# A hybrid attention and linear-attention step on one core: output projection in 512-column chunks, token groups outermost, each product split into two 64-row halves

## The reference, cut to what matters

```
def merge(x, o_attn, ga, o_gla, gg, gla_norm_g, w_out):
    o_gla = rmsnorm(o_gla...)
    mix = jnp.concatenate([o_attn * jax.nn.silu(ga), o_gla * jax.nn.silu(gg)], axis=-1)
    return x + mix @ w_out
```

## Time and profile before

| what | value |
|---|---|
| time, median of 3 runs | 2030.36 us (2029.29 to 2030.73) |
| profiled execution: span from first to last instruction | 2029.8 us |
| mean granted TensorE clock | 0.987 of full speed |
| PE busy | 1937.9 us (95% of the span), 12160 products |
| DVE, ACT, POOL busy | 835.3, 447.5, 640.0 us |
| DMA | 184.43 MB, mean 91 GB/s |

### The profile page before, as it was taken

How to read it: one execution, slowest core, us unless ns; L and a number is a source line. 1 busy time by engine, 2 the same in 40 slices (tenths; PEclk the granted TensorE clock), 3 DMA queues, 4 the chain that set the end, 5 groups by cost and what they waited for, 6 DMA issues and landing times.

```text
span 2029.8 us, 33101 instructions
## 1 busy us (share of the span) xinstructions
PE 1937.9 (95%) x12160; PEld 1809.8 (89%) x12160; DVE 835.3 (41%) x1553; ACT 447.5 (22%) x1064; POOL 640.0 (32%) x509
## 2 busy tenths in 40 slices
PE   5999999989999999999999999999999899999999
PEld 4899999867777779999988888889999899999999
DVE  6454453134334331111277777875555640000000
ACT  6211111133333331000244344441001120000000
POOL 1433333111112222233334434332323333333331
PEclk8999999989999999999999999999999999999999
DMA  6322222222222322221322222333433472222221
GB/s 214 128 65 65 65 65 75 78 69 75 71 68 75 96 64 88 71 71 56 92 76 84 75 83 75 86 96 120 143 110 107 142 233 88 88 86 81 86 88 34
DMA packets 237665, 184.43 MB, mean 91 GB/s; under 512 B 15345, under 2 KB 236017, under 8 KB 236178
## 3 DMA queue, kind: packets, MB, share of 16 engines
q1 hardware_dynamic: 159618, 131.99, 21.3%
q10 hardware_dynamic: 78000, 51.81, 9.1%
HBM read 133.27 MB, written 52.31 MB: 91 GB/s over the span
## 4 chain that ended last, share of the span: by engine, by line
PE 77%; DVE 13%; issue 4%; ACT 3%; DMA 2%; ACTq 1%; DVEq 0%; POOL 0%; SPq 0%; POOLq 0%
PE p L1557 14%; PE p L1559 14%; PE p L1558 14%; PE p L1631 7%; PE p L1632 7%; PE p L1633 7%; DVE xn L1723 4%; PE p L504 2%; PE p L487 2%; ACT work L551 2%; PE p L713 2%; PE p L497 2%; DVE work L627 1%; DVE work L613 1%; PE p L724 1%
## 5 line engine op out<-in xcount | busy, mean ns | idle before, releaser
L1557 PE MATMUL p<-x_hi,w_lo 128*128 128x384 f32 x2112 | 730.9, 346 | 0.0
L1559 PE MATMUL p<-x_hi,w_hi 128*128 128x384 f32 x2112 | 708.5, 335 | 0.0
L1558 PE MATMUL p<-x_lo,w_hi 128*128 128x384 f32 x2112 | 708.2, 335 | 0.0
L450 POOL TENSOR_TENSOR w_hi<-raw,small 128x512 fp32r<-128x512 f32 x176 | 186.3, 1059 | 870.9 <-PE p L1559 859.6
L1557 PEld LDWEIGHTS p<-x_hi,w_lo 128*128 128x128 f32 x2112 | 398.2, 189 | 41.6 <-issue 39.2
L1558 PEld LDWEIGHTS p<-x_lo,w_hi 128*128 128x128 f32 x2112 | 398.4, 189 | 0.4
L1559 PEld LDWEIGHTS p<-x_hi,w_hi 128*128 128x128 f32 x2112 | 397.8, 188 | 0.0
L1631 PE MATMUL p<-w_hi,x_lo 128*128 128x256 f32 x1152 | 328.2, 285 | 5.7 <-DVE x_lo L1796 5.7
L1632 PE MATMUL p<-w_lo,x_hi 128*128 128x256 f32 x1152 | 327.9, 285 | 0.0
L1633 PE MATMUL p<-w_hi,x_hi 128*128 128x256 f32 x1152 | 327.7, 284 | 0.0
L455 POOL TENSOR_TENSOR w_lo<-raw,w_hi 128x512 fp32r<-128x512 f32 x176 | 228.6, 1299 | 13.8
(11 more groups left out here) (181 smaller groups left out, 1842.7 us busy)
## 6 DMA issues: line engine op xcount, KB each, us to landing
raw<-in_w_in SPq DMA_DIRECT2D x176, 256.0 KB, 3.7
h_t<-xn SPq DMA_DIRECT2D x132, 192.0 KB, 1.9
raw<-in_w_out SPq DMA_DIRECT2D x32, 512.0 KB, 3.6
work<-h_t ACTq DMA_DIRECT2D x42, 256.0 KB, 5.2
out<-work ACTq DMA_DIRECT2D x76, 128.0 KB, 2.9
work<-h_t SPq DMA_DIRECT2D x24, 384.0 KB, 4.1
work<-h_t ACTq DMA_DIRECT2D x17, 512.0 KB, 5.6
work<-in_x_prompt SPq DMA_DIRECT2D x64, 128.0 KB, 3.5
```

The lines of the kernel that those rows point to most:

```text
L450: pool.tensor_tensor(w_hi[:, k:k + 4, 0:n], w_raw(k, n), zeros[:, :].unsqueeze(1) .to_broadcast([P, 4, n]), ALU.add).then_inc(s_whi, 1)
L1557: pe.matmul(out, w_lo[:, k, :], x_hi[:, k, tok], start=(k == 0), stop=False)
L1558: pe.matmul(out, w_hi[:, k, :], x_lo[:, k, tok], start=False, stop=False)
L1559: mm = pe.matmul(out, w_hi[:, k, :], x_hi[:, k, tok], start=False, stop=(k == KT - 1))
```

## The change: what it does

The chunk is 512 columns wide, so there are 4 chunks. The token groups are outermost: for each group of 384 tokens (three tiles) all 4 chunks are run, 12 group-chunks g in all, and the weights are loaded and split three times. The loads are per contraction slice: 128 x 512, 256 KB, in four slots, 192 loads. ACT makes the high part and DVE the low part, POOL has no more work here. Each product of 128 rows is issued as two of 64 rows, the lower and the upper half of the partitions, each into a PSUM bank of its own; a tile takes two banks, a group-chunk six, and they rotate over all eight. DVE adds first the one bank and the residual, then the other bank. The stores go through SP's queue, between the loads. All engines' code of this part is written out, without loops. The pieces of the activations come in the order of the groups: eight for the first group at the start, eight each for the second and third during g = 1 and g = 5.

```
-WCH = 256
+WCH = 512
+NGRP = NG * NCH
...
-            return [(q, n, i) for q in range(4) for n in range(NG) for i in range(2)]
+            return [(q, n, i) for n in range(NG) for q in range(4) for i in range(2)]
...
+        HALVES = [slice(0, P // 2), slice(P // 2, P)]
+        def half_bank(g, t, half):
+            return banks[(3 + 2 * NG * g + 2 * t + half) % 8][:, 0:WCH]
+        def piece_after(g, k):
+            if g % NCH == 1 and g // NCH + 1 < NG and 4 <= k < 12:
+                return 8 * (g // NCH + 1) + k - 4
+            return None
...
+                for k in range(4):
+                    load_w_out(0, k)
+                for t in range(NG):
+                    load_x_res(0, t)
+                load_pieces(4, 7)
                 store_last(0)
                 store_last(1)
-                load_pieces(4, 6)
+                load_pieces(7, 8)
...
+                for g in range(NGRP):
+                    for k in range(4 if g == 0 else 0, KT):
+                        load_w_out(g, k)
+                        if g == 0 and k == 5:
+                            store_last(2)
+                        if g > 0 and k == 6:
+                            for t in range(NG):
+                                store_y(g - 1, t)
+                                load_x_res(g, t)
+                        if piece_after(g, k) is not None:
+                            load_pieces(piece_after(g, k), piece_after(g, k) + 1)
...
+            def high_w(g, k):
+                u = 16 * g + k
+                act.wait_ge(t_w[k % 4], 16 * (u // 4) + 16)
+                if u < 4:
+                    act.wait_ge(s_wfree, 4 * N_ITEMS + (k + 5))
+                else:
+                    act.wait_ge(t_wfree, 2 * u - 6)
+                act.activation(o_hi[k % 4], o_raw[k % 4], ACT.Copy).then_inc(t_whi, 1)
...
-            high(0, 6)
+            high(0, 7)
+            for k in range(4):
+                high_w(0, k)
+            high(7, 8)
             item_silu(N_ITEMS, 2)
...
+            def out_chunk(n, g):
+                for b in range(4):
+                    for t in range(NG):
+                        if b == 0:
+                            pe.wait_ge(t_y, NG * g + (t + NG))
...
+                        for i in range(4):
+                            k = 4 * b + i
+                            if t == 0:
+                                pe.wait_ge(t_wlo, 16 * g + (k + 1))
+                                if k % 2 == 0:
+                                    pe.wait_ge(t_mlo, SLOTS + 8 * n + k // 2 + 1)
+                            for half, rows in enumerate(HALVES):
+                                pe.matmul(out[half], x_lo[rows, k, tok], o_hi[i][rows], start=(k == 0), stop=False)
+                            for half, rows in enumerate(HALVES):
+                                pe.matmul(out[half], x_hi[rows, k, tok], o_lo[i][rows], start=False, stop=False)
+                            for half, rows in enumerate(HALVES):
+                                mm = pe.matmul(out[half], x_hi[rows, k, tok], o_hi[i][rows], start=False,
+                                               stop=(k == KT - 1))
+                                if t == NG - 1:
+                                    mm.then_inc(t_wfree, 1)
+                                elif k == KT - 1:
+                                    mm.then_inc(t_acc, 1)
...
+            for g in range(NGRP):
+                for k in range(4 if g == 0 else 0, KT):
+                    if g > 0 and k == 0:
+                        add(g - 1, 0)
+                        add(g - 1, 1)
+                    low_w(g, k)
+                    if g > 0 and k == 3:
+                        add(g - 1, 2)
+                    if piece_after(g, k) is not None:
+                        low(piece_after(g, k), piece_after(g, k) + 1)
```

More of the change, by code:

```diff
@@ L241, in project @@
         t_mlo = sem("t_mlo")
-        t_w = [sem(f"t_w{i}") for i in range(2)]
+        t_w = [sem(f"t_w{i}") for i in range(4)]
         t_whi = sem("t_whi")
-        t_wready = sem("t_wready")
+        t_wlo = sem("t_wlo")
         t_wfree = sem("t_wfree")
-        t_x = [sem(f"t_x{i}") for i in range(NT)]
+        t_x = [sem(f"t_x{i}") for i in range(NG)]
         t_acc = sem("t_acc")
         t_y = sem("t_y")
+        t_y0 = sem("t_y0")
         t_st = [sem(f"t_st{i}") for i in range(3)]
@@ L367, in out_loads @@
                 sp.wait_ge(s_wready, 4 * (N_ITEMS + 1))
[L368 to L369 removed]
+                for k in range(4):
[3 more added lines that the diff above has]
+                load_pieces(4, 7)
                 store_last(0)
                 store_last(1)
[L372 removed]
+                load_pieces(7, 8)
                 sp.dma_start(o_dec, o_t[D_MODEL // 2:D_MODEL, SEQ:TOK].rearrange("(k p) n -> p k n", p=P))\
                   .then_inc(t_dec, 16)
[L375 to L388, removed]
+                for g in range(NGRP):
[10 more added lines that the diff above has]
+                for t in range(NG):
+                    store_y(NGRP - 1, t)
+                for t in range(NG):
+                    sp.wait_ge(t_st[t], 16 * NGRP)
             def store_item(j, row, n_rows, gates=None):
@@ L1394, in _ @@
                 split(pool, j)
[L1396 to L1409, removed]
         @block.scalar
@@ L1614, in _ @@
             pe.wait_ge(sl_og, 4 * NT + 1)
[L1615 to L1624, removed]
-                        for i in range(4):
[L1626 to L1638, removed]
@@ new lines, in out_chunk @@
+            def out_chunk(n, g):
+                for b in range(4):
+                    for t in range(NG):
+                        if b == 0:
+                            pe.wait_ge(t_y, NG * g + (t + NG))
+                        out = [half_bank(g, t, half) for half in range(2)]
+                        tok = slice(n * TN + t * P, n * TN + t * P + P)
+                        for i in range(4):
+                            k = 4 * b + i
[14 more added lines that the diff above has]
+                                    mm.then_inc(t_acc, 1)
@@ L1640, in _ @@
+            for n in range(NG):
+                for c in range(NCH):
+                    out_chunk(n, NCH * n + c)
         @block.vector
@@ L1809, in _, with low_w @@
-            dve.sem_inc(t_y, NT)
-            low(0, 6)
-            silu_g(N_ITEMS, 2)
[L1812 to L1817, removed]
+            def low_w(g, k):
+                dve.wait_ge(t_whi, 16 * g + k + 1)
+                if g == 0 and k < 4:
+                    dve.wait_ge(s_wfree, 4 * N_ITEMS + (k + 5))
+                dve.tensor_tensor(o_lo[k % 4], o_raw[k % 4], o_hi[k % 4].bitcast(F32), ALU.subtract)\
+                   .then_inc(t_wlo, 1)
@@ new lines, in add @@
+            def add(g, t):
+                if t == NG - 1:
+                    dve.wait_ge(t_wfree, 2 * (16 * g + KT))
+                else:
+                    dve.wait_ge(t_acc, 2 * ((NG - 1) * g + (t + 1)))
+                dve.wait_ge(t_x[t], 16 * g + 16)
+                if g > 0:
+                    dve.wait_ge(t_st[t], 16 * g)
+                dve.tensor_tensor(y_sb[:, t, :], half_bank(g, t, 0), x_res[:, t, :], ALU.add).then_inc(t_y0, 1)
+                dve.wait_ge(t_y0, NG * g + t + 1)
+                dve.tensor_tensor(y_sb[:, t, :], half_bank(g, t, 1), y_sb[:, t, :], ALU.add).then_inc(t_y, 1)
@@ new lines, in _ @@
+            dve.sem_inc(t_y, 2 * NG)
+            low(0, 7)
+            for k in range(4):
+                low_w(0, k)
+            low(7, 8)
+            silu_g(N_ITEMS, 2)
+            for g in range(NGRP):
+                for k in range(4 if g == 0 else 0, KT):
+                    if g > 0 and k == 0:
[4 more added lines that the diff above has]
+                        add(g - 1, 2)
+                    if piece_after(g, k) is not None:
+                        low(piece_after(g, k), piece_after(g, k) + 1)
@@ L1820, in hybrid_step @@
+            for t in range(NG):
+                add(NGRP - 1, t)
 def hybrid_step(nc, x_p, x_s, cache_k, cache_v, state, norm_g, w_in, w_up, b_gate, qg, kg, sinks, gla_g, w_out,
```

53 lines of the change are left out of this document (21 added, 32 removed).

## The result

The changed kernel takes 2064.57 us (median of 4 runs, 2060.75 to 2068.36), the kernel before 2029.82 beside it; the ratio is 1.0173, 95% interval 1.0153 to 1.0192. I had forecast 2014 us and a range up to 2046. The forecast had the wrong sign. One of the 13 executions of the kernel before that were taken beside three of the later runs took 3133.99 us at a mean granted clock of 0.556, and is left out of the ratios.

The account below looks back on a forecast made before the run. PE's product pace was taken to bound the kernel. Pace -41.5, start -1.8, pieces +16.3, clock +4.5, eighth slice +4.5 and end +1.3 sum to -16.7 from 2029.8: 2014 us forecast, range 1998 to 2046.

Parts of the forecast that it names:

- The pace: Output projection products: halves run side by side, 1728 pairs at 0.216 us take 373.2 us, 41.5 us less.
- my first rival: Output projection products: the fixed 0.0133 us stays on a pair, pace only 23.0 less, 2026 us; chance 0.25.
- The eighth slice: Chunk changes: its late load costs 0.5 us at nine changes, 4.5 us, plus 1.7 us twice in chunks with pieces.
- The clock: Blocks with pieces: three gaps over 2 us are each followed by low clock costing 1.5 us, 4.5 us together.
- The blocks with pieces: g = 1 and g = 5: pieces on DVE delay weight slots; 16.3 us, including 1.7 twice at the eighth slice.
- the gated block: Fourth block with pieces, which DVE multiplies, ACT casts and DVE subtracts: 2.85 us a slot, 6.3 us of waits.
- The end: After the last product: two adds instead of one and a store of twice the size, 1.3 us more.
- The start: Start of the output projection: PE starts 5.4 us after it was free, plus 3 us low clock; 1.8 us less.
- Late refills at every block: Start of each of 48 blocks: slot refill chain exceeds 0.28 us slack; at 0.7 us a block 2047 us; chance 0.18.
- no overlap: Output projection: halves of an fp32r product do not overlap, 3456 x 0.216 = 746 us, about 2350 us; chance 0.03.

Follow-up runs that it names:

- stores later: Changed kernel with three stores and three residual loads issued behind the eighth weight slice's load instead of ahead of it: 2024.58 us, ratio 0.998 to the kernel before.
- half of the queue: Changed kernel with only the three residual loads ahead of the eighth weight slice's load, the three stores behind it: 2032.22 us, ratio 1.0017 to the kernel before.
- one half alone: The kernel with stores later, pieces spread, with products of the lower half alone, contraction rows 64 to 127 left out: 2349.14 us in one execution.
- stores later, pieces spread: Stores later, plus 16 pieces of the second and third token group behind every fourth weight slice in two group-chunks each: 2005.97 us, ratio 0.9895.

## Why the prediction was wrong, step by step

**The pace** was the first wrong step. I took 0.216 us for a pair, "the nearest row in form", and it is 0.2267. The products of the earlier trace rows were like the new ones in their halves, those of the earlier trace rows in their type. In all rows here the fixed part goes with the type: fp32r pays 0.0133 at 256, 384 and 512 columns, at 128 rows and at 64. Why it does is open. The step was off by 18.5 us; this was my first rival, and with it alone I had 2026. The Trainium skill's formula ("TensorE: Matmul & The Clock Gate", section "Back-to-back issue gap") would give 0.2158 here; the trace does not agree. My own working with the two weight loads of a pair one after the other does not show either: they lie within 0.19 us (timeline).

```profile
1870.17 0.19 PEld L1655 LDWEIGHTS p<-w_hi,x_hi 64*128 64x128 f32 x2
```

**The eighth slice** was the larger one, and the one that turned the sign. The mechanism was named: its load stands behind the last add, three stores and three loads on SP. Its size was not: 7.9 us forecast, 30.2 measured. I issued it at 11.7 us after the start of the last block and landed it 2.9 to 3.7 us later; the eleven were issued at 12.6 to 14.5 and landed 5.4 to 9.4 later. In the gap whose chain is shown, the block began some 18.4 us ahead of 1889.0, when the eighth slice was due (two blocks and three slices at 0.2267), at 1870.6: the load is issued 12.8 us after it, and takes 5.92. The issue is late by another way than mine. I had SP wait for the last of the three adds and then issue two transfers. The last add ends at 11.1, before its store's turn at 11.5: what takes the time is the six transfers one after another behind slice 6, 3.3 us from 9.5 on. Each microsecond beyond the slack is paid eleven times. I had written "more if the 1.5 MB ahead of it are not through", took 0.5 us for nine changes, and gave the range only 1.5 us; it is 1.5 to 3.1 there, and 5.0 and 4.1 in the two chunks with pieces. The runs with the stores later and with half of the queue show this cause: issued at 9.85 us, the slice came in time, although it still took 5.1 us to land.

**The clock** was the same mechanism again: eleven gaps instead of three could drop it. It did so behind five of the eleven and at the gated pieces, for 15.1 us instead of 4.5. With the gaps at the eighth slice gone, 4.8 are left.

**The blocks with pieces** were about right: 10.0 us against 12.9 (11.35 with their share at the eighth slice), the gated block 5.6 against 6.3, and they went when the pieces were moved behind the fourth slice. **The end** was right. **The start**: the first gap was 6.7 us against 5.4, counted as in the prediction from the end of the input projection. Nearly all of the difference is the load of the seventh piece (number 6), which landed 4.7 us after its issue where I had taken 3.5. (The links that I listed behind it add up to 0.6 less than the time that I gave; DVE takes the low part of that piece first, and from landing to PE it measured 2.8 us against 2.7.) The seventh weight slice, behind a store that waits for silu, cost 1.7 us that I had not seen.

**Late refills at every block**, my rival for the slower side, did not happen. The whole stage has no wait at an ordinary block, so the chain of cast, subtraction and wake-up stayed within its slack. The slower pace had widened that slack, by my own chain from 0.28 to about 0.4 us (an estimate: 36 pairs less 26 at 0.2267, less the chain of 1.88), so the forecast 0.28 was not put to the test. The range was too narrow because I bounded the one recurring DMA wait from the lowest and median landing times, 2.9 and 3.7 us, although the same row went up to 10.7. The time of the **no overlap** rival, about 2350, is also a wrong sum: 746 instead of 373.2 us gives 2387 by the same terms, or about 2362 with the added waits gone. That the run with one half alone took 2349 us is chance: nothing of that rival was in it.

## What to carry to other kernels

- Of two kinds of rows near a new instruction, one like it in shape and one like it in type, both are ends of the range; the price must not be taken from one.
- In an in-order DMA queue, put loads that feed the engine which sets the pace ahead of stores and of loads with time to spare. Here, moving six transfers by one place was worth 40 us (2064.6 to 2024.6). Size such a wait by the issue time of all that stands ahead (about three quarters of the delay here) and by landing times from the same dense part, and multiply it by how often it comes.
- Work for a later stage goes behind the last of a burst of refills, not between them: 18.6 us here (2024.6 to 2006.0).

## What the runs showed of the hardware

- Two 64-row halves of an fp32r product run side by side, but take as long as one of 128 rows: 0.68 us for three in both. Splitting a full-height product gave nothing.
- A gapless stream of 64-row products in one array half had its clock granted at 0.50 (1.2 GHz) for 690 us. The same stream with the other half beside it (stores later, pieces spread) ran at 1.00. PE had no gap in either. The first rests on one execution.
- The fixed 0.0133 us of an fp32r product is there at 2.4 GHz alone: at the low clock, 512 columns take 0.427 us, and 256 take 0.213 in the kernel before (its timeline behind the first gap):

```profile
1604.90 0.41 PE L1633 MATMUL p<-w_hi,x_hi 128*128 128x256 f32 x1
1605.12 0.41 PE L1631 MATMUL p<-w_hi,x_lo 128*128 128x256 f32 x1
1605.33 0.41 PE L1632 MATMUL p<-w_lo,x_hi 128*128 128x256 f32 x1
```

- A gap of 2.4 to 3.1 us lowered the clock behind it in some cases and not in others. After the one that follows the product of 1923.3 us (2.9) PE ran on with pairs 0.23 us apart, the full clock; after the one behind 1959.0 (3.0) they came 0.43 apart, the low one (changed kernel):

```profile
1926.76 0.39 PE L1653 MATMUL p<-w_lo,x_hi 64*128 64x512 f32 x2
1926.99 0.40 PE L1655 MATMUL p<-w_hi,x_hi 64*128 64x512 f32 x2
...
1962.57 0.63 PE L1653 MATMUL p<-w_lo,x_hi 64*128 64x512 f32 x2
1963.00 0.63 PE L1655 MATMUL p<-w_hi,x_hi 64*128 64x512 f32 x2
```
